# Gate statistics transposed into columns, and modulation units summed along rows on VectorE

## The reference

```python
# modulation: six vectors of 1024 from one conditioning vector c, for each layer
mod = silu(c) @ w_ada + b_ada            # 6144 columns
h   = rms_norm(x, g) * (1 + scale) + shift
# token mixing: one projection of 10 column groups, then two bidirectional scans
g = (p[..., OFF_ML_G:OFF_GLA_Q] + b_gates)          # input and forget gates, 4 heads, 2 directions
b = cumsum(chunk(log_sigmoid(f)))                   # within a chunk
d = where(causal, b[:, None] - b[None, :] + li[None, :], -inf)
m = maximum(b + m_prev, max(d, -1))                 # running-max stabiliser
s = (q @ k.T) * exp(d - m);  h = (s @ v + a * q @ C) / maximum(abs(den), exp(-m))
```

## Time and profile before

| | |
|---|---|
| median of 3 runs | 1331.14 us (1329.98 to 1332.6) |
| profiled execution, its own time | 1330.0 us |
| its span, first to last instruction | 1328.3 us |
| TensorE busy, matmuls | 1254.5 us, 94% of the span |
| VectorE busy | 937.4 us, 71% |
| ScalarE busy | 764.8 us, 58% |
| mean granted TensorE clock | 0.977 of full speed |
| HBM traffic | 246 GB/s over the span |

### The profile page before, as it was taken

The page is one execution under the profiler, slowest core; times in us unless marked ns, Lnnn a source line. Parts: engine busy times, 40 slices in busy tenths (PEclk is TensorE's granted clock), DMA queues, the critical chain, the costliest instruction groups (busy, mean ns, idle before and its releaser), DMA issues.

```text
span 1328.3 us, 18911 instructions
## 1 busy us (share of the span) xinstructions
PE 1254.5 (94%) x7127; PEld 1081.5 (81%) x7127; DVE 937.4 (71%) x1097; ACT 764.8 (58%) x906; POOL 115.6 (9%) x129
## 2 busy tenths in 40 slices
PE   5998999999999999999995799999999999999994
PEld 3787888998988999778884688888888888888883
DVE  5757311487577751785446888888888888988887
ACT  6544211574315453862333377777777777777785
POOL 1100000110000000040000111111111110011024
PEclk9999989999999999999997899999999999999997
DMA  9861330342455210323216699999999999999994
GB/s 376 279 158 35 125 98 1 87 130 92 175 216 220 98 64 33 144 79 144 79 64 253 253 371 349 406 393 398 401 403 402 399 397 397 393 395 398 388 322 201
DMA packets 77659, 319.35 MB, mean 240 GB/s; under 512 B 6568, under 2 KB 31176, under 8 KB 47832
## 3 DMA queue, kind: packets, MB, share of 16 engines
q1 hardware_dynamic: 70336, 290.14, 55.5%
q0 software_dynamic: 7264, 28.40, 8.6%
HBM read 291.15 MB, written 35.75 MB: 246 GB/s over the span
## 4 chain that ended last, share of the span: by engine, by line
PE 82%; DVE 9%; ACT 4%; DMA 3%; issue 1%; SPq 0%; POOLq 0%; POOL 0%; DVEq 0%; ACTq 0%
PE psum L2627 37%; PE psum L2234 7%; PE psum L2563 7%; PE psum L2292 3%; PE psum L2293 3%; PE psum L2294 3%; PE psum L2323 1%; PE psum L2325 1%; PE psum L2324 1%; PE psum L2375 1%; DMA raw<-w_in_units 1%; DMA xs<-x 1%; PE psum L2376 1%; PE psum L2650 1%; PE psum L2644 1%
## 5 line engine op out<-in xcount | busy, mean ns | idle before, releaser
L2000 DVE TENSOR_TENSOR e_lo<-e_raw,e_hi 128x2048 fp32r<-128x2048 f32 x192 | 432.8, 2288 | 44.4 <-ACT e_hi L1317 44.4
L1317 ACT ACTIVATE e_hi<-e_raw 128x2048 fp32r<-128x2048 f32 x192 | 365.8, 1916 | 82.9 <-PE psum L2627 82.0
L2627 PE MATMUL psum<-e_hi,xt_hi 128*128 128x512 f32 x496 | 153.4, 390 | 0.1
L2627 PE MATMUL psum<-e_lo,xt_hi 128*128 128x512 f32 x496 | 152.9, 389 | 0.0
L2627 PE MATMUL psum<-e_hi,xt_lo 128*128 128x512 f32 x496 | 152.8, 389 | 0.0
L2627 PEld LDWEIGHTS psum<-e_hi,xt_hi 128*128 128x128 f32 x496 | 92.7, 188 | 20.1 <-DVE xt_lo L2004 0.5
L2627 PEld LDWEIGHTS psum<-e_lo,xt_hi 128*128 128x128 f32 x496 | 93.1, 188 | 19.5
L2627 PEld LDWEIGHTS psum<-e_hi,xt_lo 128*128 128x128 f32 x496 | 93.1, 188 | 19.5
L2292 PE MATMUL psum<-w_hi,h_hi 128*128 128x256 f32 x352 | 101.3, 288 | 0.0
L2293 PE MATMUL psum<-w_hi,h_lo 128*128 128x256 f32 x352 | 100.3, 285 | 0.0
L2294 PE MATMUL psum<-w_lo,h_hi 128*128 128x256 f32 x352 | 100.3, 285 | 0.0
(11 more groups left out here) (427 smaller groups left out, 2374.0 us busy)
## 6 DMA issues: line engine op xcount, KB each, us to landing
e_raw<-w_e_units SPq DMA_DIRECT2D x192, 1024.0 KB, 7.5
ada_x<-w_ada_units SPq DMA_DIRECT2D x16, 1024.0 KB, 4.8
raw<-w_in_units SPq DMA_DIRECT2D x13, 1024.0 KB, 7.0
ada_raw<-w_ada_units SPq DMA_DIRECT2D x8, 1024.0 KB, 21.9
bc<-rows_dram SPq DMA_DIRECT2D x16, 512.0 KB, 3.8
xs<-x SPq DMA_DIRECT2D x4, 1024.0 KB, 10.5
acc_dram<-zero_r SPq DMA_DIRECT2D x1, 4096.0 KB, 20.3
wo_raw<-w_out SPq DMA_DIRECT2D x4, 1024.0 KB, 6.0
```

Source lines behind the costliest of these rows:

```text
L1317: act.activation(e_hi[u % EH][:], e_raw[u][:], ACT.Copy).then_inc(e_hi_ok, 1)
L2000: dve.tensor_tensor(e_lo[u][:], e_raw[u][:], e_hi[u % EH][:], ALU.subtract).then_inc(e_lo_ok, 1)
L2627: m = pe.matmul(o[:, BANK * b:BANK * (b + 1)], x[:, k, :], w[:, D * j + BANK * b:D * j + BANK * (b + 1)], start=a, stop=z)
```

## The change

Gate statistics: the fourth exponential writes partitions 64 to 127 of row_a, so that one transpose turns two statistics of a chunk; ten transposes of row_a and ten of 36 partitions of row_m stand behind the first five k blocks of tile 7. They go to banks 2, 3, 6 and 7. VectorE gathers cst from them with 8 copies, between its low splits of v0 and v1. The first tap of conv tile 4 moves ahead of the exponentials on ScalarE, its other taps ahead of the low split of unit 11 on VectorE. The v product waits for 7 convolved tiles and not for 8. Tile 2 doesn't wait for g_free.

Modulation: the 16 later units come from the host as transposed rows, output channels on the partitions and all 1024 input channels along the row. SP loads silu's argument c as a row broadcast to 128 partitions, in the place that o0's weights leave; ScalarE applies silu to it between the sigmoids of o0 and the split of unit 17. VectorE multiplies and sums in two instructions per unit, straight into modc. TensorE's ones-column products, mod_acc and ada_cols are gone for these units.

```diff
-        modps = psum[:, 7 * BANK:7 * BANK + 12 * KC].rearrange("p (j r) -> p j r", r=2)
+        STAT_CHUNKS = (4, 4, 2)
+        def stat_af(g):
+            b = (2, 3, 6)[g]
+            return psum[:, b * BANK:(b + 1) * BANK].rearrange("p (c n) -> p c n", n=P)
+        stat_m = psum[:, 7 * BANK:7 * BANK + 36 * TA].rearrange("p (c n) -> p c n", n=36)
...
 SP
             for n in range(O0 + 1, len(STREAM)):
                 load_unit(n)
+                if n == O0 + 2:
+                    wait_used(sp, O0)
+                    sp.dma_start(c_row[:], I["c_row"].to_broadcast([P, D])).then_inc(c_row_full, 16)
...
 POOL
-            pool.memset(one_c[:], 1.0)
...
 ScalarE
             conv_first(3, 1, 1, True)
+            conv_first(4, 1, 2, True)
             act.wait_ge(row_dve, 1)
             act.activation(rows32[:, 1, :], rows32[:, 1, :], ACT.Exp).then_inc(row_act, 1)
-            act.activation(row_f[:], row_f[:], ACT.Exp).then_inc(row_act, 1)
+            act.activation(row_a[64:P, :], row_f[0:64, :], ACT.Exp).then_inc(row_act, 1)
...
             conv_silu(3, 1, 1)
-            conv_first(4, 1, 2, True)
...
-            act.wait_ge(num_mm, 2 * TL)
-            act.activation(c_mod[:], cc, ACT.Silu).then_inc(c_again, 1)
...
             o_gates(0)
+            act.wait_ge(c_row_full, 32)
+            act.activation(c_row[:], c_row[:], ACT.Silu).then_inc(c_again, 1)
             split_hi(17)
...
 VectorE
+            conv_taps(4, 1, 2)
             split_lo(11)
-            conv_taps(4, 1, 2)
...
             split_lo(13)
+            dve.wait_ge(stat_mm, 1)
+            for g, n in enumerate(STAT_CHUNKS):
+                for q in range(2):
+                    v = stat_af(g)[:, 0:n, 64 * q:64 * q + 64].rearrange("p c (d x) -> p c d x", d=2)
+                    dve.tensor_copy(cst[:, q, 4 * g:4 * g + n, :].rearrange("p c (d h) -> p c d h", d=2), v[:, :, :, 0:NH])
+            for d in range(2):
+                i = dve.tensor_copy(cst[:, 2, :, NH * d:NH * d + NH], stat_m[:, :, 32 * d:32 * d + NH])
+            i.then_inc(stat_ready, 1)
             split_lo(14)
             conv_taps(8, 0, 2)
             conv_taps(9, 0, 3)
-            dve.wait_ge(stat_mm, 1)
-            dve.tensor_copy(cst[:].rearrange("p q c s -> p (q c s)"), psum[:, 7 * BANK:7 * BANK + 3 * TA * 2 * NH]).then_inc(stat_ready, 1)
...
             def ada_column(j):
+                if j == ADA_REST[0]:
+                    dve.wait_ge(c_again, 1)
                 dve.wait_ge(ada_x_full[j % 2], 16 * ((j - ADA_REST[0]) // 2 + 2))
-                if j >= ADA_REST[4]:
-                    dve.wait_ge(ada_cols, j - 3)
-                o, w = mod_acc[:, j % 4, :], ada_x[j % 2]
-                link(dve.tensor_scalar(o, w[:, 0, :], c_mod[:, 0, 0:1], None, ALU.mult))
-                for k in range(1, KC):
-                    i = dve.scalar_tensor_tensor(o, w[:, k, :], c_mod[:, k, 0:1], o, ALU.mult, ALU.add)
-                    if k < KC - 1:
-                        link(i)
+                for r in range(2):
+                    w = ada_x[j % 2][:, r, :]
+                    i = dve.scalar_tensor_tensor(w, w, 1.0, c_row[:], ALU.mult, ALU.mult, accum_out=modc[:, 2 * j + r, 0:1])
                 i.then_inc(ada_acc, 1)
...
-            ada_columns(8, 9)
             split_lo(17)
             for q in range(4):
                 o_pair(1, q)
+                if q < 2:
+                    ada_columns(8 + q)
...
-            dve.wait_ge(ada_cols, 24)
-            link(dve.tensor_tensor(modc[:, 2 * KC:, :], modps[:, 2 * KC:, :], b2, ALU.add))
+            dve.wait_ge(ada_acc, acc_count(23))
+            link(dve.tensor_tensor(modc[:, 2 * KC:, 0], modc[:, 2 * KC:, 0], col("b_ada")[:, 2 * KC:], ALU.add))
...
 TensorE
+            def t_unit(n, i0, has_ctx, free, behind=None):
...
-                    if free is not None:
+                    if free is conv_free or free is g_free and j:
                         pe.wait_ge(free, i0 + j - 1 - (2 if free is conv_free else 0))
...
+            def stat_rows(k):
+                if k == 0:
+                    pe.wait_ge(row_act, 4)
+                if k >= TA // 2:
+                    return
+                for c in (2 * k, 2 * k + 1):
+                    pe.transpose(stat_af(c // 4)[:, c % 4, :], row_a[:, P * c:P * (c + 1)], ident[:])
+                    i = pe.transpose(stat_m[:, c, :], row_m[0:36, P * c:P * (c + 1)], ident[0:36, 0:36])
+                if k == TA // 2 - 1:
+                    i.then_inc(stat_mm, 1)
+            t_unit(11, 6, False, conv_free, stat_rows)
             t_unit(12, 8, False, conv_free)
-            pe.wait_ge(row_act, 4)
-            (the 30 products with sel_s)
...
-            pe.wait_ge(conv_free, 8)
+            pe.wait_ge(conv_free, 7)
             pe.wait_ge(stat_ready, 1)
...
                 if p == 1:
+                    pe.wait_ge(conv_free, 8)
                     pe.wait_ge(conv_act, 8)
...
-            def acc_to_cols(name):
-                (2 products with one_c for each unit; called for o1, gk, gq, gv0, gv1)
...
 host
+def ada_rows_of(w):
+    return np.ascontiguousarray(w.T.reshape(-1, 2, P, D).transpose(0, 2, 1, 3).reshape(-1, P, 2 * D))
```

More of the change, by code:

```diff
@@ L153, in build @@
         one_s = small("one_s", [P, 2])
-        one_c = small("one_c", [P, 2])
         zero_r = small("zero_r", [P, P])
@@ L171, in build @@
         vv_lo = at("vv_lo", AT_RING + 8 * KB, [P, 3, KC, UW], F32R)[:, 0:3:2, :, :]
-        ada_x = [at(f"ada_x{s}", AT_RING + (16 + 8 * s) * KB, [P, KC, UW]) for s in range(2)]
-        mod_acc = at("mod_acc", AT_OUT + 58 * KB, [P, 4, UW])
+        ada_x = [at(f"ada_x{s}", AT_RING + (16 + 8 * s) * KB, [P, 2, D]) for s in range(2)]
+        c_row = at("c_row", AT_OUT + 58 * KB, [P, D])
         xs = at("xs", AT_OUT, [P, TA, D])
@@ L604, in unit_src @@
             if kind == "ada":
+                if j >= ADA_REST[0]:
+                    return I["w_ada_rows"][j - ADA_REST[0]].rearrange("p (r k) -> p r k", r=2)
                 return I["w_ada_units"][j].rearrange("p (k n) -> p k n", k=KC)
@@ L2240, in t_tile @@
                 return last
-            def t_unit(n, i0, has_ctx, free):
+            def t_unit(n, i0, has_ctx, free, behind=None):
                 unit_ready(n)
                 for j in range(2):
-                    if free is not None:
+                    if free is conv_free or free is g_free and j:
                         pe.wait_ge(free, i0 + j - 1 - (2 if free is conv_free else 0))
-                    last = t_tile(i0 + j, n, j, has_ctx)
+                    last = t_tile(i0 + j, n, j, has_ctx, behind if j else None)
                     if j == 0:
@@ L2253, in _ @@
             t_unit(10, 4, True, conv_free)
-            t_unit(11, 6, False, conv_free)
-            t_unit(12, 8, False, conv_free)
-            pe.wait_ge(row_act, 4)
-            for q, src in enumerate((row_a, row_f, row_m)):
-                for c in range(TA):
-                    o = 7 * BANK + (q * TA + c) * 2 * NH
-                    last = pe.matmul(psum[:, o:o + 2 * NH], src[:, P * c:P * (c + 1)], sel_s[:], start=True, stop=True)
-            last.then_inc(stat_mm, 1)
+            def stat_rows(k):
[9 more added lines that the diff above has]
+            t_unit(11, 6, False, conv_free, stat_rows)
+            t_unit(12, 8, False, conv_free)
             def tok_unit(name, n, x_hi, x_lo, t0, behind=None):
@@ L2382, in _ @@
             pe.wait_ge(c_done, N_STEPS)
-            def acc_to_cols(name):
-                for j in ADA_BEHIND[name]:
-                    pe.wait_ge(ada_acc, acc_count(j))
-                    for r in range(2):
-                        i = pe.matmul(modps[:, 2 * j + r, :], mod_acc[:, j % 4, P * r:P * (r + 1)], one_c[:], start=True, stop=True)
-                    i.then_inc(ada_cols, 1)
             def z_part(i):
@@ L2430, in behind_r0 @@
                 if j == 0:
-                    acc_to_cols("gv1")
                     ctx_transposes(0)
@@ L2458, in _ @@
             pe.wait_ge(z_out, 10)
-            acc_to_cols("gq")
             tok_unit("gv0", 19, h_hi, h_lo, 0)
-            acc_to_cols("gv0")
             tok_unit("gv1", 20, h_hi, h_lo, 0)
@@ L2789, in arrays_of @@
         "x": np.ascontiguousarray(a["x"][0]), "ctx": np.ascontiguousarray(a["ctx"][0]),
-        "small": small_array(a), "w_ada_units": ada_units(a["w_ada"][0]),
+        "small": small_array(a), "w_ada_units": ada_units(a["w_ada"][0][:, 0:UW * ADA_REST[0]]),
+        "w_ada_rows": ada_rows_of(a["w_ada"][0][:, UW * ADA_REST[0]:]), "c_row": np.ascontiguousarray(a["c"]),
         "w_in_units": w_in_units, "w_out": np.ascontiguousarray(a["w_out"][0]), "pos_row": pos_row, "pos_col": pos_col,
```

6 lines of the change are left out of this document (1 added, 5 removed).

## The result

The changed kernel takes 1309.64 us (median of 4 runs, 1305.9 to 1310.69) against 1330.56 for the kernel before (4 runs, 1328.79 to 1332.6). The ratio is 0.9837, with a 95% interval of 0.9813 to 0.9862. The forecast was 1308.3 in a range of 1306 to 1313. The profiled execution of the changed kernel took 1309.47 us, with a span of 1307.7 us and a mean granted clock of 0.983.

A forecast was written before the change was run, and what follows sets the result against it. TensorE, busy 94% of the span and carrying 82% of the chain, bounds the kernel. Gains of 16.1 (gate statistics) and 6.7 (modulation), 22.8 together, take 1330.0 to 1307.2; the median lies 1.1 above: 1308.3, range 1306 to 1313.

The forecast's parts named there:

- place B: Projection units o1 to r0, 325 to 486 us: removed ones-column blocks and a clock spell gain 5.17 + 1.49 = 6.7 us.
- Steps 1 to 4: 124 to 197 us: gap before q tile 6 (4.28), its spell (2.30), sel_s block and copy (10.23), low-clock tail (1.53) go.
- Step 5: Tile 7: 20 added transposes at 0.11 us each cost 2.2; changing between kinds could add 0.5.
- Step 6: VectorE's 8 small copies, 1.3 us between v0's and v1's splits, stay covered, with 9 us before the v product.
- Step 7: Tile 2 without its g_free wait gains nothing; the gap before tile 4 grows from 0.88 to about 2.5 us.
- the clock rival: The longer gap before tile 4, or tile 7's transposes, brings a new clock fall costing 1.9 us: 1310.2; chance 0.27.
- A spell of 0.50 before tile 4's 96 us: Sign of a wrong forecast: granted clock at 0.50, that is 1.2 GHz, before k tile 4.
- Steps 8 and 9: gk, gv0 and gq product blocks leave TensorE (5.17 us), o1's and gv1's count 0; spell behind tile 13 goes (1.49).
- Step 10: VectorE's modulation sums: two 1024-column instructions per unit at 1.35 us each, at most 2.4, off the path.
- Step 11: c_row's load lands in 3.8 us; its silu makes ScalarE some 3 us late until o1's gates, at no cost.
- The slower rival: VectorE bounds o1 to r0 if 49 + 32x exceeds 155 + 16, from x = 3.8 us a sum; chance 0.02.

The follow-up runs named there:

- e4: The changed kernel with conv tile 4's first tap and other taps back in their old places; 1313.72 us, ratio 0.9888.
- e5: The changed kernel with the 20 transposes grouped by kind, row_a's first and then row_m's, instead of alternating; 1307.81 us, ratio 0.9835.
- e10: The changed kernel with row_m transposed from all 128 rows instead of 36, still alternating with row_a's; 1307.06 us, ratio 0.9828.
- e7: The changed kernel with 8 short unread products put back behind o1 and 8 ahead of the context key transposes, in gv1's place; 1309.83 us, ratio 0.9852.
- e8: The changed kernel with 16 short unread products put back at each of the places of gk's, gq's and gv0's blocks; 1313.46 us, ratio 0.9877.
- e3: The kernel before with only the modulation part of the change; 1323.69 us, ratio 0.9959.
- e9: The changed kernel with each summed VectorE instruction run four times; 1380.84 us, ratio 1.0385.

## Why the prediction was right, and where it was off

In profiled time the forecast was 22.8 less, and 20.6 came. The difference: transposes -2.55, the spell at tile 4 -1.41, the spell behind the scan that stayed away +1.62, place B +0.37, start-up and the rest -0.4, and 0.2 that I can't place. Step by step:

- *Steps 1 to 4* (gap, spell, block, tail) held. Their sum can be read from the piece up to the scan: 16.1 less 2.55 for the transposes and 1.41 for tile 4's spell is 12.14, against 12.34 measured. e4 shows the gap's and the spell's share alone. The scan came 11.5 us earlier and not 16.
- *Step 5, the transposes, was mis-sized*: 2.2 (at most 2.7) forecast, 4.75 measured. I scaled a uniform group of eight and priced the change between kinds at 0.1 in each of five places. It is some 0.14 for each change between a 36-row and a 128-row operand, of which there are twenty (e5, e10): 10 x 0.12 + 10 x 0.07 + 20 x 0.14 = 4.7. The low bound for a short one was worked out wrong too: 0.12 us for 256 columns, scaled to 36, is 0.02 and not 0.03.
- *Step 6* held: eight copies in 0.9 us, ahead of v1's last split, which ended 9 us before v began.

```profile
162.10 0.64 DVE L1599 COPY cst<-psum 128x32 f32<-128x32 f32 x6
162.66 0.30 DVE L1601 COPY cst<-psum 128x40 f32<-128x40 f32 x2
163.30 2.29 DVE L1456 TENSOR_TENSOR vv_lo<-v_raw,vv_hi 128x2048 fp32r<-128x2048 f32 x1 [0.34 <-ACT vv_hi L891]
```

- *Step 7 and the clock rival*: the gap became 2.59 as forecast (2.5), and the clock fell behind it, at the place that the rival named, for 1.4. "A spell of 0.50 before tile 4's 96 us" was one of the forecast's own signs of being wrong, and it came: the claim that the new gap costs nothing failed, though the time stayed in the range. The chance of 0.27 was too low: with such a gap it fell in 6 of 8 profiles. Against it stands a spell that the forecast kept and that stayed away in this execution, behind the scan (1.62). So the time is right partly by luck: two errors of the clock cancel, and with the second spell it would have been 1.6 us more.
- *Steps 8 and 9* held: gk 1.79 (1.68), gq, gv0 and the spell 5.24 (1.81 + 1.68 + 1.49 = 4.98); o1's and gv1's blocks count nothing (e7). Sum of place B 7.03 against 6.66. The spell of step 9 is not certain before either (e8).
- *Step 10* held: 1.22 and 0.08 for the read of the accumulator. They overlap, and the next sum starts 1.15 us behind the one before (336.61 and 337.76), against 1.35 taken.

```profile
L1687 DVE SCALAR_TENSOR_TENSOR ada_x<-ada_x,c_row x32: 1215/1220/1226, 336.6 to 456.4; 128x1024 f32<-128x1024 f32 x32
L1687 DVE DVE_READ_ACCUMULATOR ada_x<-ada_x,c_row x32: 79/83/85, 337.8 to 457.5; 128x1 f32 x32
```

Here the Trainium skill's rule of half rate ("Vector Engine (DVE) Microarchitecture Reference", section "Points that are easy to get wrong") and the measurement differ: with both sources fp32 in SBUF and the sum beside, the instruction is no slower than L1728 without a sum, 1.28, nor by the column than the split at 163.30 above (2.29 for 2048 columns). The measurement decides.

- *Step 11* held: c_row landed in time for the silu at 328.14, 2.77 us after ScalarE was free for it, and the gates of o1 were as paced by TensorE as before (e3's 49.14 for o0 and o1).

```profile
324.08 1.28 ACT L1190 ACT_TABLE_LOAD   x1
328.14 1.06 ACT L1190 ACTIVATE c_row<-c_row 128x1024 f32<-128x1024 f32 x1 [2.77 <-DMA c_row<-c_row]
```

- *The slower rival* had its mechanism right and its threshold too high (e9). By its formula VectorE at 1.15 + 3 x 1.27 = 4.96 us a sum would end 37 us after the kernel before; the context keys came 51 after it (536.91 against 486.02). In the changed kernel they stand 20.8 ahead of those of before, so they come later than before from 1.15 + (49 + 20.8) / 32 = 3.3 us a sum, an estimate, and not from 3.8. The formula gave VectorE all of the stretch, without the time in which it must wait for splits and products whatever its load.

## What to carry to other kernels

Price a product or transpose put between others by its neighbours' shape, not only by its own: here twenty transposes that alternate between 36 and 128 rows cost twice what twenty full ones did, and padding or grouping got 2.2 to 2.4 us back. When a small block leaves an engine's queue, look at what ends the wait behind it: in front of a wait that ends by itself the block was free, elsewhere it was worth its own length. Where the clock may fall, give a spell a chance and an average price, and compare pieces between two fixed instructions over several profiles; a removed wait can lengthen the next one into the range where it falls.

## What the runs showed of the hardware

- A change between a transpose with a 36-row stationary operand and a product with a 128-row one costs TensorE some 0.14 us, at full clock; a short one among its like takes 0.07, a full one 0.12 (estimates from e5, e10 and the changed kernel). Alternating source tiles and PSUM banks adds nothing.
- The same idle time before the same work is followed by half clock in some executions and not in others: after 2.0 to 3.4 us in 6 of 8, after 4.3 to 4.6 us in 3 of 3, after 0.86 to 1.13 us in none of 5, behind the scan in 5 of 13. A spell costs 1.4 to 1.7 us (2.3 before tile 6 in the kernel before).
- Twenty transposes among dense matmuls didn't lower the clock: 1.00 from 124 to 150 us.
- Multiply and sum over 1024 fp32 columns takes VectorE 1.22 us and 0.08 for the read of the sum; of several in a row one starts every 1.15 us.
